# Two gate column groups of a SwiGLU as a third unit of seven quarter products, with Silu on ACT

## The reference

```python
x = x + rmsnorm(mixed, post_mix_g[l])
h = rmsnorm(x, pre_ffn_g[l])
f = (jax.nn.silu(h @ w_ffn_gate[l]) * (h @ w_ffn_up[l])) @ w_ffn_down[l]
x = x + rmsnorm(f, post_ffn_g[l])
```

## Time and profile before

| | us |
|---|---|
| median of 3 runs | 803.73 |
| lowest and highest | 803.61, 803.79 |
| span of the profiled execution | 801.8 |
| PE busy | 791.1 (99%) |
| DVE busy | 602.1 (75%) |
| ACT busy | 459.6 (57%) |

### The profile page before, as it was taken

The page is one execution under the profiler, slowest core; times in us unless marked ns, Lnnn a source line. Parts: engine busy times, 40 slices in busy tenths (PEclk is TensorE's granted clock), DMA queues, the critical chain, the costliest instruction groups (busy, mean ns, idle before and its releaser), DMA issues.

```text
span 801.8 us, 10515 instructions
## 1 busy us (share of the span) xinstructions
PE 791.1 (99%) x4242; PEld 665.8 (83%) x4242; DVE 602.1 (75%) x603; ACT 459.6 (57%) x591; POOL 70.5 (9%) x135
## 2 busy tenths in 40 slices
PE   7999999999999999999999999999999999999997
PEld 5897898888888888888889889988888888888885
DVE  6799897557689888667489859965567896985762
ACT  5568976554456555535455698865436556465341
POOL 5530000000220000000011100000003100000000
PEclk9999999999999999999999999999999999999999
DMA  9868444546388786962476745434654769769501
GB/s 286 256 225 259 137 143 145 179 136 210 121 298 240 224 309 173 262 213 103 157 226 221 263 130 184 160 108 165 215 196 148 280 176 305 208 221 262 209 1 54
DMA packets 84276, 156.48 MB, mean 195 GB/s; under 512 B 7314, under 2 KB 27906, under 8 KB 84228
## 3 DMA queue, kind: packets, MB, share of 16 engines
q1 hardware_dynamic: 79728, 147.42, 54.2%
q0 software_dynamic: 4224, 8.39, 6.2%
q10 hardware_dynamic: 276, 0.01, 0.0%
HBM read 154.75 MB, written 1.05 MB: 194 GB/s over the span
## 4 chain that ended last, share of the span: by engine, by line
PE 96%; issue 1%; DMA 1%; ACT 0%; DVE 0%; SPq 0%; POOL 0%; DVEq 0%; POOLq 0%
PE work L776 14%; PE work L778 14%; PE work L777 14%; PE acc L776 9%; PE acc L778 9%; PE acc L777 9%; PE work L768 4%; PE work L769 4%; PE work L770 4%; PE work L862 3%; PE work L863 3%; PE work L864 3%; DMA weights_raw<-in_w_in 1%; PE work L966 1%; PE acc L890 1%
## 5 line engine op out<-in xcount | busy, mean ns | idle before, releaser
L1563 DVE TENSOR_TENSOR weights_lo<-weights_raw,weights_hi 128x2048 fp32r<-128x2048 f32 x114 | 260.6, 2290 | 89.6 <-ACT weights_hi L1178 89.5
L1178 ACT ACTIVATE weights_hi<-weights_raw 128x2048 fp32r<-128x2048 f32 x116 | 221.7, 1915 | 152.7 <-PE work L778 74.2
L776 PE MATMUL work<-weights_hi,act_a_hi 128*128 128x512 f32 x416 | 164.1, 394 | 0.0
L778 PE MATMUL work<-weights_hi,act_a_lo 128*128 128x512 f32 x416 | 162.3, 390 | 0.0
L777 PE MATMUL work<-weights_lo,act_a_hi 128*128 128x512 f32 x416 | 161.9, 389 | 0.0
L776 PE MATMUL acc<-weights_hi,act_b_hi 128*128 128x512 f32 x240 | 94.7, 394 | 0.0
L778 PE MATMUL acc<-weights_hi,act_b_lo 128*128 128x512 f32 x240 | 93.6, 390 | 0.0
L777 PE MATMUL acc<-weights_lo,act_b_hi 128*128 128x512 f32 x240 | 93.4, 389 | 0.0
L778 PEld LDWEIGHTS work<-weights_hi,act_a_lo 128*128 128x128 f32 x416 | 78.1, 188 | 16.6
L776 PEld LDWEIGHTS work<-weights_hi,act_a_hi 128*128 128x128 f32 x416 | 78.1, 188 | 16.3 <-issue 0.8
L777 PEld LDWEIGHTS work<-weights_lo,act_a_hi 128*128 128x128 f32 x416 | 78.2, 188 | 15.7
(11 more groups left out here) (225 smaller groups left out, 1248.2 us busy)
## 6 DMA issues: line engine op xcount, KB each, us to landing
weights_raw<-in_w_in SPq DMA_DIRECT2D x43, 1024.0 KB, 5.2
weights_raw<-in_w_ffn_gate SPq DMA_DIRECT2D x16, 1024.0 KB, 6.6
weights_raw<-in_w_ffn_up SPq DMA_DIRECT2D x12, 1024.0 KB, 5.5
weights_raw<-in_w_ffn_down SPq DMA_DIRECT2D x12, 1024.0 KB, 4.9
weights_raw<-in_w_pa SPq DMA_DIRECT2D x8, 1024.0 KB, 5.0
weights_raw<-in_w_pb SPq DMA_DIRECT2D x8, 1024.0 KB, 5.0
weights_raw<-in_w_o SPq DMA_DIRECT2D x8, 1024.0 KB, 6.1
q_feat<-in_w_ffn_down SPq DMA_DIRECT2D x6, 1024.0 KB, 8.6
```

Source lines behind the costliest of these rows:

```text
L776: mm(dst, xh, wh, start=first, stop=False)
L778: return mm(dst, xl, wh, start=False, stop=final)
L1178: activate(w_hi[:, SLOT[n], :], raw_slot(RAWS[n]), ACT.Copy).then_inc(hi_done.sem, 1)
L1563: v.tensor_tensor(w_lo[:, SLOT[n], :], raw_slot(RAWS[n]), bits(w_hi[:, SLOT[n], :]), ALU.subtract).then_inc(split_done.sem, 1)
```

## The change

- The gate groups 3 and 4 are made as a unit of their own, between the two up units. `s` 7 to 13 now belong to it and `s` 14 to 20 to the up groups 3 and 4. The panels `fg` 6 to 9 go. The plan has 76 panels for 73.
- The work banks are given out anew: the gate unit has banks 0 and 1, and the transposes of groups 1 and 2 both have banks 2 and 3.
- silu is one ACT instruction, Silu, that writes its result; DVE's half of it and the factors of two go, and so do two small POOL operations in each layer.
- `x_whole` is copied by ACT from the transposes of x (x_whole_part), where DVE added hi and lo. Whoever claims a bank of these transposes also waits for that copy.
- k_tok and k_feat become one buffer, which serves as a sixth raw buffer once the sums of x are split. The fourth block of unit 0 is loaded into it.
- The transposes of groups 1, 2 and 3 stand after `s` 7, after `s` 8 and in the middle of `fgu` 1.

```diff
+UNITS = (("up", 1), ("gate", 3), ("up", 3))
...
-    plan += [("fg", 6), ("fg", 7), ("s", 7), ("s", 8), ("down", 2), ("s", 9), ("down", 3), ("fg", 8), ("s", 10)]
-    plan += [("fg", 9), ("s", 11), ("down", 4), ("s", 12), ("down", 5), ("s", 13)]
-    plan += [("fgu", 0), ("fgu", 1), ("down", 6)]
+    plan += [("s", 7), ("s", 8), ("down", 2), ("s", 9), ("s", 10), ("down", 3), ("s", 11), ("s", 12), ("down", 4)]
+    plan += [("s", 13), ("s", 14), ("down", 5), ("s", 15), ("s", 16), ("fgu", 0), ("s", 17), ("s", 18), ("s", 19)]
+    plan += [("s", 20), ("fgu", 1), ("down", 6)]
...
-    uses += two("fg", 6, 0) + two("turn_f", 2, 2) + [(("sa", 1), 2), (("sb", 1), 3)] + two("turn_f", 4, 0)
-    uses += [(("sd", 1), 3)] + two("fg", 8, 0)
+    uses += [(("sa", 1), 0)] + two("turn_f", 2, 2) + [(("sb", 1), 1)] + two("turn_f", 4, 2) + [(("sd", 1), 1)]
+    uses += [(("sa", 2), 2), (("sb", 2), 3), (("sd", 2), 3)]
     uses += two("fgu", 0, 0) + two("turn_f", 6, 2) + two("turn_f", 8, 2) + [(("turn_f", 10), 0)]
...
+        k_both = sb("k_tok_and_feat", [P, 2 * NT * 4 * P])
+        KTOK = k_both[:, 0:NT * 4 * P].rearrange("p (t g d) -> p t g d", t=NT, g=4)
...
+        KT = k_both[:, NT * 4 * P:].rearrange("p (g s) -> p g s", g=4)
+        f_silu_tail = sb("silu_tail", [P, NT, 256])
...
+            if s == RAW + 2:
+                return k_both[:, :]
...
-        SLOTS = RAW + 2
+        SLOTS = RAW + 3
...
-                    (s < RAW or i >= LOADS.index(("b", 0)) + (0, 2)[s - RAW])]
+                    (s < RAW or i >= LOADS.index(("b", 0)) + (0, 2, 4)[s - RAW])]
...
-        TURNED_AT = {("fg", 2): 0, ("fg", 6): 1, ("s", 8): 2, ("fgu", 0): 3, ("fgu", 1): 4}
+        TURNED_AT = {("fg", 2): 0, ("s", 7): 1, ("s", 8): 2, ("s", 20): 3, ("fgu", 1): 4}
...
+                    elif slot == RAW + 2:
+                        sp.wait_ge(*xs_split.at(l, 4))
...
-            def half_rstd_of(n, ready, count, count2):
-                pool.wait_ge(*ready)
-                nc.gpsimd.tensor_tensor(ms_eps[:, n:n + 1], mean_sq[:, n:n + 1], eps4_t[:, :],
-                                        ALU.add).then_inc(pool_step, 1)
-                pool.wait_ge(pool_step, count)
-                nc.gpsimd.tensor_tensor(rstd[:, n:n + 1], ms_eps[:, n:n + 1], mhalf[:, :],
-                                        ALU.pow).then_inc(pool_step, 1)
-                pool.wait_ge(pool_step, count2)
-                t = (n - 3) // 2
-                nc.gpsimd.tensor_tensor(half_r2[:, t:t + 1], rstd[:, n:n + 1], rstd[:, n:n + 1],
-                                        ALU.mult).then_inc(rstd_done.sem, 1)
 
...
+                    if before[0] == "h":
+                        pe.wait_ge(*xs_copied.at(l, before[1] + 1))
...
-                        elif name == "fg" and (j // 2) % 2 == 1:
-                            turn_f(j // 4)
-                        elif name == "fgu":
+                        elif (name, j) == ("fg", 3):
+                            turn_f(0)
+                        if (name, j) == ("fgu", 1):
+                            split_ready(n)
+                            t_panel_product(name, j, gate_banks[0], xn_hi, xn_lo, 0)
                             turn_f(GROUPS - 2)
-                        t_product(name, j, gate_banks, xn_hi, xn_lo)
-                        if (name, j) == ("fgu", 1):
+                            t_panel_product(name, j, gate_banks[1], xn_hi, xn_lo, 1).then_inc(panel_used.sem, 1)
                             turn_f(GROUPS - 1)
+                        else:
+                            t_product(name, j, gate_banks, xn_hi, xn_lo)
...
-                        if j == 8:
-                            turn_f(2)
+                        if j in (7, 8):
+                            turn_f(j - 6)
...
-                def silu_tanh(c, t):
-                    name, width = ("fg", 512) if c < GROUPS else ("fgu", 256)
-                    sig, n = multiplied(name, c % GROUPS if c < GROUPS else 0, t)
-                    act.wait_ge(*sig.at(l, n))
-                    if c:
-                        act.wait_ge(*f_gate.at(l, 2 * c + t - 1))
+                def silu(c, t):
+                    if c == 3 and t:
+                        act.wait_ge(*panel_used.at(l, AT["s", 13] + 1))
+                        gate = bank("sa", 1)[:, :]
+                    elif c in (3, 4):
+                        act.wait_ge(*s_added.at(l, 4 if c == 3 else 5 + t))
+                        gate = p1_t if c == 3 else p5_t if t else u2_t
+                    else:
+                        name, width = ("fg", 512) if c < GROUPS else ("fgu", 256)
+                        sig, n = multiplied(name, c if c < GROUPS else 0, t)
+                        act.wait_ge(*sig.at(l, n))
+                        gate = bank(name, 2 * c + t if c < GROUPS else t)[:, 0:width]
                     if c == 0:
                         act.wait_ge(*rstd_done.at(l, 2 + 2 * t))
-                    ps = bank(name, 2 * c + t if c < GROUPS else t)[:, 0:width]
-                    done(activate(f_th_t[:, t, 0:width], ps, ACT.Tanh, scale=rstd[:, 3 + 2 * t:4 + 2 * t]),
-                         f_th, 2 * c + t + 1)
+                    if c in (2, 3, 4):
+                        act.wait_ge(*f_up.at(l, PRODUCT[c - 2, t]))
+                    out_t = f_silu_t[:, 2 * (c % 2) + t, :] if c < GROUPS else f_silu_tail[:, t, 0:256]
+                    done(activate(out_t, gate, ACT.Silu, scale=rstd[:, 3 + 2 * t:4 + 2 * t]), f_gate, GATE[c, t])
+                def x_whole_part(t):
+                    for h in range(2):
+                        act.wait_ge(*xa_done.at(l, 4 + 2 * t + h + 1))
+                        done(activate(x_whole[:, 4 * h:4 * h + 4, P * t:P * t + P], four(bank("h", 2 * t + h)[:, :]),
+                                      ACT.Copy), xs_copied, 2 * t + h + 1)
 
                 def x_sums_hi():
...
+                        x_whole_part(0)
...
+                    if name == "s" and UNITS[j // 7][0] == "gate" and j % 7 in UNIT_DONE_AT:
+                        even, t = UNIT_DONE_AT[j % 7]
+                        silu(UNITS[j // 7][1] + even, t)
...
+                        x_whole_part(1)
...
-                def silu(c, t):
-                    if c > 1:
-                        dve.wait_ge(*f_up.at(l, PRODUCT[c - 2, t]))
-                    dve.wait_ge(*f_th.at(l, 2 * c + t + 1))
-                    ps = bank("fg", 2 * c + t)[:, :] if c < GROUPS else bank("fgu", t)[:, 0:256]
-                    w = 512 if c < GROUPS else 256
-                    done(v.scalar_tensor_tensor(f_silu_t[:, 2 * (c % 2) + t, 0:w], f_th_t[:, t, 0:w], 1.0, ps,
-                                                ALU.add, ALU.mult), f_gate, 2 * c + t + 1)
...
-                    own(v.tensor_tensor(x_whole, bits(xn_hi[:, :, :]), bits(xn_lo[:, :, :]), ALU.add))
+                    dve.wait_ge(*xs_copied.at(l, 4))
...
-                    if name == "s" and j % 7 in UP_AT:
-                        c, t = UP_AT[j % 7]
-                        f_product(2 * (j // 7) + c, t)
+                    if name == "s" and j % 7 in UNIT_DONE_AT:
+                        kind, c = UNITS[j // 7]
+                        even, t = UNIT_DONE_AT[j % 7]
+                        if kind == "up":
+                            f_product(c + even, t)
+                        elif j % 7 != 6:
+                            unit_add(j // 7, 1 - even, t)
```

More of the change, by code:

```diff
@@ L404, in trunk @@
         PRODUCT = {p: n + 1 for n, p in enumerate(PRODUCTS)}
+        GATES = [(c, t) for c in range(3) for t in range(NT)] + [(3, 0), (4, 0), (4, 1), (3, 1), (GROUPS, 0), (GROUPS, 1)]
+        GATE = {p: n + 1 for n, p in enumerate(GATES)}
         FREED_BY = {"xn": (xa_done, 0), "u": (u_done, 0), "gates": (gates_done, 0),
@@ L459, in for_layers, with unit_block @@
                 layer(DEPTH - 1, False, True)
+        def unit_block(l, u, what):
+            kind, c = UNITS[u]
+            c, k = 512 * (c + what // 2), 512 * (what % 2)
+            return (w_ffn_up if kind == "up" else w_ffn_gate)[l][k:k + 512, c:c + 512]
         block = ctx.enter_context(nc.Block())
@@ L678, in layer @@
                     if m == 4:
-                        for u in range(2):
+                        for u in range(NU):
                             pool.wait_ge(*summed.at(l, 2 * u + 1))
@@ L684, in layer @@
                     step += 1
-                    if n in (3, 5):
-                        half_rstd_of(n, ms_done.at(l, m + 1), l * 10 + step, l * 10 + (step + 1))
-                        step += 1
-                    elif last and n == 7:
+                    if last and n == 7:
                         pool.wait_ge(tail_summed, 1)
@@ L1397, in unit_copy @@
                     if u:
-                        act.wait_ge(*f_up.at(l, PRODUCT[2 * u, 1] if i == 2 else PRODUCT[2 * u - (i == 0), 0]))
+                        read, m = unit_read(u - 1, i > 0, i == 2)
+                        act.wait_ge(*read.at(l, m))
                     elif i == 2:
```

(1 more changed line is left out.)

87 lines of the change are left out of this document (38 added, 49 removed).

## The result

The changed kernel takes 840.75 us (median of 4 runs, 839.14 to 844.28), the kernel before 803.72. The ratio is 1.0466, 95% interval 1.0453 to 1.0478. Forecast were 832.0 us and 820 to 840. The profiled execution took 842.1 us, its span is 840.3 (801.8 before).

The account below looks back on a forecast made before the run. PE, busy 99% of the span, was taken as the bound. Per layer, -2.5 us of removed work plus waits (a) to (g) gave +14.15, 28.3 for both: 803.7 + 28.3 = 832.0 us, range 820 to 840.

Parts of the forecast that it names:

- Rival 1: PE loses its clock in the long wait at the second transposes, so `down` 2 runs slower: 837 us, chance 0.22.
- (g): `s` 20 waits for the addition after `s` 19, which stands behind splits on DVE: 3.65 us per layer.
- Removed: Four gate panels (21.8 us of PE) go and a unit (19.3) comes: 2.5 us less per layer.
- (a): Start of the FFN: ACT's `x_whole` copies and the table load delay `fu` splits and Silu; PE waits 2.45 us per layer.
- (b): `fg` 4: the fourth block is issued only after the sums of x are split and lands late; wait 0.9 us.
- (c): `s` 6 waits for the addition after product 5, behind a split and block sum of `s` 7 on DVE: 1.0 us.
- (d), (e): Transposes of groups 1 and 2: PE waits for DVE's product, then for the two shared banks; 6.3 us per layer together.
- (f): `s` 16 takes the bank of `s` 15, freed by an addition behind the split of `s` 17: wait 2.35 us.
- Rival 4: The table load before Silu also has a drain, holding ACT 1.4 us longer: 834.8 us, chance 0.04.
- rival 5: Later waits shrink, as each PE wait gives DVE and ACT time for the next: 822 us, chance 0.18.
- Rivals 2 and 3: 2: banks and additions ready in time, 798.7 us, chance 0.04; 3: only the FFN start costs, 803.6 us, chance 0.02.

Follow-up runs that it names:

- The control with zeros: The kernel before, nothing of the change in it, with 110 products of zeros added into the output sums at three places of each FFN: 828.62 us.
- The new order: The changed kernel with `down` 5 moved between `s` 15 and `s` 16, and `fgu` 0 between `s` 19 and `s` 20: 828.91 us.

## Why the prediction was wrong, and where it was right

The sign and the mechanism were right. Each term of the sum is within 0.3 us of the table above, and all of them with the unit came to 28.1 us for both layers (28.3 forecast). The step that failed is the clock. The sum held every matmul at 2.4 GHz. Rival 1 (chance 0.22) had the drop, but at one place, the transposes and `down` 2, and there its 2.5 us per layer were near: 1.9 and 2.4. The other place, `s` 20 and the half of `fgu` 1 behind it, took 2.7 and 3.0 more, `s` 16 0.1. That is 10.1 us in all, and 801.8 + 28.1 + 10.1 + 0.2 for the start is 840.2, the span (840.3). The median of the runs is 1.4 below the profiled one. The four runs lie 5 us apart at granted clocks of 0.982 to 0.989; the slowest (844.28) has 0.984 and the profiled one 0.982, so the clock's share alone does not rank them, and only one of the four has a trace.

Three errors stand in that step. The wait of (g), 3.65 us, was in the sum, and the rival did not ask what it does to the clock. (The numbers in (g) add up to 379.2 and not 379.3, so the wait was 3.5 by them; measured were 3.6.)

The evidence against was misread. The prediction saw no drop behind the 3.9 us at the start, because the granted clock prints as 1.00 there. The durations say otherwise. The first two rows are from the kernel before, eight transposes behind that wait and eight a little later; the next three are from the changed kernel, matmuls of 512 columns, two to a row but for the last:

```profile
7.25 1.97 PE L748 MATMUL work<-identity,q_tok 128*128 128x128 f32 x8
13.13 1.31 PE L748 MATMUL work<-identity,q_tok 128*128 128x128 f32 x8 [0.99 <-DVE q_tok L1605]
```

```profile
10.72 0.98 PE L987 MATMUL acc<-weights_lo,act_a_hi 128*128 128x512 f32 x2
11.54 0.62 PE L987 MATMUL acc<-weights_hi,act_a_lo 128*128 128x512 f32 x2
12.00 0.39 PE L987 MATMUL acc<-weights_hi,act_a_hi 128*128 128x512 f32 x1
```

On PE's timeline the transposes behind the wait start 0.21 us apart, those from 13.13 on 0.11. The pair of matmuls at 10.72 takes 11.54 - 10.72 = 0.82 us until the next pair starts, that at 11.54 takes 0.46. So PE ran at about half its speed at the start of both kernels, and the printed 1.00 is no reading of it. Whether the clock had fallen in that wait or had never risen before it, no run shows; but it is no evidence against a drop.

Last, the page that speaks of it, the Trainium skill (TensorE: Matmul & The Clock Gate, Part 1), which has an idle PE go to half its clock, was put aside as shown by no row. Between matmuls the rows before could not show it, as PE never stopped there. Here the trace agrees: the granted clock is 0.50 in every stretch behind a wait of 4.4 us or more.

Point by point:
- Removed: 2.5 us per layer, as worked out. The control with zeros (828.62 for 828.6) shows the same for added matmuls: PE's list grows by what they take.
- (a) 2.40. The place of the copies is 2.0 of it, the table load 1.1 (they overlap).
- (b) 0.72 and 1.16. It lies with the sixth buffer: without it the wait is gone.
- (c) 1.00.
- (d), (e) 6.23. The length was right, the reason half: it is the place of the subtraction in DVE's list, not the banks.
- (f), (g) 2.37 and 3.63. The new order took about 3.6 us per layer of them, and 4.6 us of slow clock in both together (840.75 - 828.91 - 7.2).
- Rival 4 (the drain) did not come true, and neither did rival 5: (f) and (g) are as long as in the sum. Rivals 2 and 3 did not come true either, since the waits (c) to (g) are there.
- What would show it: the wait of 5.7 us, those of 2.4 and 3.6 at the last unit and Silu's end were there. PE's busy time did not fall by 5 us: it rose from 791.1 to 800.4, and most of that is the 10.1 us of slow matmuls, which count as busy. That DVE would have almost no idle time was wrong too: it waited 2.04 us for ACT in the chain, and the prediction's own walk had that gap, from T + 7.5 to T + 9.4.

## What to carry to other kernels

Where PE never stops, walk the order by hand for each engine: the waits came out within 0.3 us, before any run. Then price a wait of some us twice, once for its length and once for about 2 us that the slow matmuls behind it take more. In these runs the second price was paid behind every wait of 3.7 us or more, and behind waits of 2.2 and 3.4 us in some places and not in others. And fewer products pay only if the engine that prepares their operands has the time: here seven splits, two block sums and three additions are 22 us of DVE (an estimate from 2.2 and 0.7 us each) for 19.3 of PE.
